# Inverting 64-wide blocks in a two-model kernel: five of its levels moved from pairs of 64-wide blocks to four blocks of 32 side by side

## The chip, the cores and the metric

One Trainium2 core runs the whole program in a single launch. Times are device microseconds (us). The profiled execution comes from the hardware profiler. In the text PE is TensorE, PEld its weight loads, DVE is VectorE, ACT ScalarE, POOL GpSimd.

## The reference

Two stacks follow each other on 256 tokens of width 2048, all in float32: two layers of four attention kinds, and then one layer with an RWKV-7 branch (16 heads of 64) and a gated-delta-rule branch (8 heads of 128), both run in two directions over 256 context tokens and 256 tokens, followed by gates, projections and an MLP. Only the two branches matter here. The delta rule of a chunk ends in a triangular solve:

```python
a_mat = jnp.einsum('bnhid,bnhjd->bnhij', kb, k) * decay
a_mat = jnp.where(idx[:, None] > idx[None, :], a_mat, 0.0) + jnp.eye(B_CHUNK, dtype=jnp.float32)
rhs = jnp.concatenate([v * beta[..., None], kb * jnp.exp(gc)[..., None]], axis=-1)
sol = lax.linalg.triangular_solve(a_mat, rhs, left_side=True, lower=True, unit_diagonal=True)
```

The RWKV branch has the same form once its scan is cut into chunks:

```python
# S_t = S_{t-1} diag(w_t) - (S_{t-1} kk_t) b_t^T + v_t k_t^T ;  y_t = S_t r_t
sa = jnp.einsum('bhvk,bhk->bhv', s, kk_t)
s = (s * dec_t[:, :, None, :] - sa[..., None] * b_t[:, :, None, :]
     + v_t[..., None] * k_t[:, :, None, :])
```

So the kernel needs, for each chunk of 128 tokens, the inverse of a unit triangular matrix of 128 by 128.

## The kernel before, in words

The program has five stages that follow one another, named in the code L (the first stack), P (the projections of the last layer), B (both branches), C (gates and output projection) and M (the MLP). Matrix products of L, P, C and M stream weights from memory; B works on what lies on the chip.

Stage B is made of threads: `thread_a(d)` for RWKV (eight pairs of heads, c = 0 to 7), `thread_b(d)` for the gated delta rule (eight heads h), each for the directions d = 0 and 1, and `tail_a`, `tail_b`, `base_a`, `base_b`. Each engine's program holds the same threads, and `weave.run` writes them out in turns: one step of each thread, up to its next `yield`, then the next step of each. So the order on every engine is fixed when the program is built, and an instruction that waits holds up all that stands behind it. Direction 1 of a head starts when direction 0 has done eight steps of its inverse (`weave.after(8, ...)`, `weave.until(("middle", c))`).

A step on PE leaves its result in a PSUM bank, taken in turn from the thread's ring (`DR`, two banks a direction; `ER`, one bank); DVE or ACT copies it out, and the thread's next step on PE waits for that.

`inverse` works level by level. The matrix is held as NA (its strict part, negated). X is the inverse of the diagonal blocks found so far, XP the transposed one. A level joins two blocks of width w = 1, 2, 4, ... 32 into one of 2w, and the last join makes 128. Matrices lie as n units: n = 8 for RWKV (4 chunks, 2 heads), n = 4 for the other. A unit of 128 by 128 has two diagonal blocks of 64; the upper is on partitions 0 to 63, the lower on 64 to 127, so that X takes 64 columns for each unit and all 128 partitions. The function `diagonal` issues the products of one call: for each unit and for each of the two halves a matmul 64 by 64 by 64. In the profile a float32 matmul is two MATMUL records and two LDWEIGHTS records. A level has three such calls:

- iq: NA times X. DVE then copies the wanted half of the columns into Q, under a mask (line 2146; line 2141 at level 0, whose copy goes into X at once).
- ix: XP and Q, which gives the new half of X; ACT copies it (line 1183).
- it: Q and XP, which gives the new half of XP; DVE copies it (line 2153).

POOL puts the identity back into the half of Q that DVE wrote (line 2747), with two Q buffers in turn. Level 0 has the first call alone, with an identity as right side. DVE starts an inverse by setting X and XP to the identity (line 2125) and writing the first level of XP under a mask (line 2132, one instruction for each half). Levels 0 to 5 give blocks of 64; level 6, with two calls of n matmuls each, joins them to 128 in the matrix XT, whose other blocks ACT (64 partitions) and POOL (line 2750) copy.

`region(buf, wd, side)` is the view of every second group of wd columns.

Of the kernel before, what the change touches and what calls it, by code (L numbers as in the profile page):

```python
# [35 lines left out]
for _n, _w in (("ident", 128), ("ones", 128), ("bones", 128), ("LE", 128), ("GT", 128), ("GE", 128), ("LT", 128),  # L36
               ("G1", 256), ("mask3", 384), ("permd", 128), ("permm", 128), ("Cd", 256), ("Sd", 256), ("Cm", 256),
               ("Sm", 256), ("scan", 512), ("type", 6), ("strict", 256), ("incl", 256), ("sel", 2), ("id64", 64)):
    CST[_n] = (CSTN, _w)
    CSTN += _w  # L40
MSK = {"strict": (0, 256), "incl": (256, 256), "lev": (512, 384), "xt0": (896, 64), "gla": (960, 1024)}
MSKN = 1984


def constants():
# [39 lines left out]
    ty = np.zeros((128, 6))  # L85
    for q in range(4):
        ty[:, q] = i % 4 == q
    for q in range(2):
        ty[:, 4 + q] = i % 2 == q
    put("type", ty)  # L90
    st = np.concatenate([a < b, a > b], 1)
    inc = np.concatenate([a <= b, a >= b], 1)
    put("id64", a[:, 0:1] % 64 == b[:, 0:64])
    put("sel", np.stack([i % 32 == 0, i % 32 == 1], 1))
# [5 lines left out]
    j = np.arange(32)  # L100
    r = i[:, None] % 64
    for d in range(2):
        for lv in range(6):
            w = 1 << lv
            s = (j // w) * 2 * w + d * w + j % w
            ok = (r // (2 * w) == s[None, :] // (2 * w)) & ((r // w) % 2 != (s[None, :] // w) % 2)
            m[:, 512 + (d * 6 + lv) * 32:512 + (d * 6 + lv) * 32 + 32] = ok
        tcol = 2 * j + 1 - d
        m[:, 896 + d * 32:896 + d * 32 + 32] = (r // 2 == tcol[None, :] // 2) & (r != tcol[None, :])
    for lv in range(7):  # L110
        w = 1 << lv
        m[:, 960 + lv * 128:960 + lv * 128 + 128] = (a // (2 * w) == b // (2 * w)) & ((a // w) % 2 == 0) & ((b // w) % 2 == 1)
    m[:, 960 + 896:960 + 1024] = a == b
# [126 lines left out]
def program(nc, W, WSM, LORA, PARd, CSTd, MSKd, CTX, XIN, XS, ZS, OUT):  # L240
    ctx = ExitStack()
    with ctx:
# [119 lines left out]
        with ExitStack() as st:  # L362
# [14 lines left out]
            for d in range(2):  # L377
                g = Mem()
                kb_ = alloc(1024)
                g.Kd, g.Bd = g.X, g.XP = kb_[:, 0:512], kb_[:, 512:1024]  # L380
                g.NA, g.AK, g.XT = alloc(1024), alloc(1024), alloc(1024)
                g.KK, g.Kt, g.Bt, g.RK, g.RB = [alloc(512) for _ in range(5)]
                g.Q = [alloc(512) for _ in range(2)]
# [11 lines left out]
            for d in range(2):  # L395
                g = Mem()
                g.NA, g.XT, g.dec, g.gl, g.Ke = [alloc(512) for _ in range(5)]
                g.X, g.XP = g.gl[:, 0:256], g.gl[:, 256:512]
# [5 lines left out]
            for d in range(2):  # L404
                g = G.d[d]
                g.Q = [alloc(256) for _ in range(2)]
# [4 lines left out]
            for g in R.d:  # L411
                g.Y, g.Rd = alloc(256), alloc(256)
            for g in R.d:
                g.H, g.R, g.U = [alloc(128) for _ in range(3)]
            for g in G.d:
                g.S, g.R, g.U = [alloc(128) for _ in range(3)]
            D.ab = alloc(128).rearrange("p (q n) -> p q n", q=4)
# [88 lines left out]
        def tensor(e):  # L506
# [307 lines left out]
            def inverse(tag, ring, NA, X, XP, Q, n):  # L814


                one = n == 4
                d = tag[-1]
                halves = [slice(0, 64), slice(64, 128)]
                me, other = halves[d], halves[1 - d]  # L820
# [15 lines left out]
                diagonal(bank(), NA, None, True).then_inc(*mark("pe_inv", "iq", tag, 0))  # L836
# [2369 lines left out]
```

## Time and profile before

| | us |
|---|---|
| median of 3 runs | 4343.27 |
| lowest, highest | 4336.54, 4343.53 |
| profiled execution | 4341.28 |
| its span | 4339.5 |
| PE busy (91% of the span) | 3936.5 |
| DVE, ACT, POOL busy | 1727.6, 1539.6, 1651.9 |

The page also cuts the span into 40 slices. Stage B lies at 2241 to 3335 us: there DMA is nearly at rest, and PE is busy for 955.6 of 1094 us.

Stage B repeats itself with a period of 133 us, in which two RWKV inverses and two of the other kind are made, one for each direction. Stage B holds 16 inverses of each kind.

### The profile page before, as it was taken

How to read it: one execution, taken by the hardware profiler on the slowest of the kernel's cores; microseconds unless marked ns; L12 is line 12 of the kernel's file. 1: busy time of each engine (PE TensorE's matmuls, PEld its weight loads, DVE VectorE, ACT ScalarE, POOL GpSimd, SP SyncE). 2: the span in 40 equal slices, each digit the busy share in tenths (PEclk: the TensorE clock that was granted, in tenths of full speed). 3: DMA queues.
4: the chain of work that ended last, by engine and by line, in shares of the span. 5: the costliest groups of instructions: out<-in, count | busy, mean ns of one | idle time of the engine just before them, and what ended most of it. 6: DMA issues, size and time to landing. Idle time of an engine off the chain costs nothing. (4 is left out here: it accounts for less than half of the span.)

```text
span 4339.5 us, 86947 instructions
## 1 busy us (share of the span) xinstructions
PE 3936.5 (91%) x37936; PEld 3563.3 (82%) x37936; DVE 1727.6 (40%) x3471; ACT 1539.6 (35%) x2630; POOL 1651.9 (38%) x1155
## 2 busy tenths in 40 slices
PE   7898998998897999999948889888898979999998
PEld 6898897887896777777737878877787979999998
DVE  2534433433433111112245565565654534333332
ACT  3333333333343222224423333333333434444442
POOL 1554453544451333335501111111112636666664
PEclk9999997999996999999969999999997979999999
DMA  4354452343442555567720000000002525555553
GB/s 154 136 184 156 165 198 105 136 175 134 153 161 95 210 206 196 216 215 271 260 72 25 25 11 16 25 24 25 6 2 112 203 95 185 181 186 179 185 184 127
DMA packets 115097, 585.17 MB, mean 135 GB/s; under 512 B 20768, under 2 KB 40096, under 8 KB 49952
## 3 DMA queue, kind: packets, MB, share of 16 engines
q1 hardware_dynamic: 114720, 579.62, 37.3%
q8 instruction: 301, 4.93, 0.5%
q14 instruction: 76, 0.62, 0.0%
HBM read 558.85 MB, written 20.71 MB: 134 GB/s over the span
## 5 line engine op out<-in xcount | busy, mean ns | idle before, releaser
L512 PE MATMUL bank<-act_L,part_L 128*128 128x256 f32 x7296 | 956.6, 291 | 1.9 <-DVE act_L L1805 1.9
L512 PEld LDWEIGHTS bank<-act_L,part_L 128*128 128x128 f32 x7296 | 916.2, 197 | 36.8 <-issue 27.5
L2639 POOL TENSOR_TENSOR part_L<-wring,part_L 128x512 fp32r<-128x512 f32 x304 | 532.6, 1753 | 657.1 <-ACT part_L L1183 656.7
L512 PE MATMUL bank<-act_P,part_P 128*128 128x512 f32 (+1 forms) x3488 | 723.2, 366 | 15.7 <-DVE act_P L2487 15.7
L512 PEld LDWEIGHTS bank<-act_P,part_P 128*128 128x128 f32 x3488 | 587.2, 188 | 176.0 <-issue 51.6
L512 PE MATMUL bank<-arena_B 64*64 64x64 f32 (+4 forms) x11456 | 542.8, 232 | 43.4 <-DVE arena_B L2255 18.5
L2639 POOL TENSOR_TENSOR part_M<-wring,part_M 128x512 fp32r<-128x512 f32 x256 | 457.3, 1797 | 307.5 <-ACT part_M L1183 307.5
L512 PEld LDWEIGHTS bank<-arena_B 64*64 64x64 f32 (+3 forms) x11456 | 469.2, 143 | 99.7 <-issue 21.7
L2639 POOL TENSOR_TENSOR part_P<-wring,part_P 128x512 fp32r<-128x512 f32 x184 | 328.3, 1789 | 471.0 <-ACT part_P L1183 471.0
L1800 DVE TENSOR_TENSOR part_L<-wring,part_L 128x512 fp32r<-128x512 f32 x304 | 219.9, 724 | 512.9 <-ACT part_L L1183 512.9
L1183 ACT ACTIVATE part_L<-wring 128x1024 fp32r<-128x1024 f32 x304 | 320.6, 1055 | 281.9 <-PE bank L512 265.3
L512 PE MATMUL bank<-act_h,part_M 128*128 128x256 f32 x3072 | 381.1, 287 | 22.8 <-DVE act_h L1805 22.8
L512 PEld LDWEIGHTS bank<-act_h,part_M 128*128 128x128 f32 x3072 | 376.3, 195 | 27.5 <-DVE act_h L1805 17.5
L512 PE MATMUL bank<-act_u,part_M 128*128 128x256 f32 x3072 | 369.3, 283 | 0.0
L512 PEld LDWEIGHTS bank<-act_u,part_M 128*128 128x128 f32 x3072 | 368.9, 192 | 0.0
L1183 ACT ACTIVATE part_M<-wring 128x1024 fp32r<-128x1024 f32 x256 | 270.2, 1057 | 267.4 <-PE bank L512 267.4
L1800 DVE TENSOR_TENSOR part_P<-wring,part_P 128x512 fp32r<-128x512 f32 x184 | 132.1, 718 | 497.1 <-ACT part_P L1183 497.1
L1800 DVE TENSOR_TENSOR part_M<-wring,part_M 128x512 fp32r<-128x512 f32 x256 | 182.2, 712 | 280.4 <-ACT part_M L1183 280.4
L1183 ACT ACTIVATE part_P<-wring 128x1024 fp32r<-128x1024 f32 x184 | 193.8, 1055 | 214.9 <-PE bank L512 214.9
L2644 POOL TENSOR_TENSOR smalls<-smalls,nhalf 128x2 f32<-128x2 f32 (+2 forms) x63 | 59.4, 943 | 378.3 <-DVE smalls L1788 378.2
L2747 POOL COPY arena_B<-cst 128x256 f32<-128x256 f32 (+1 forms) x96 | 38.0, 395 | 427.0 <-PE bank L512 427.0
L1183 ACT ACTIVATE arena_L<-bank 128x256 f32<-128x256 f32 (+2 forms) x177 | 70.6, 407 | 351.8 <-PE bank L512 291.1
(259 smaller groups left out, 4342.8 us busy)
## 6 DMA issues: line engine op xcount, KB each, us to landing
wring<-in_w SPq DMA_DIRECT2D x404, 1024.0 KB, 4.8
arena_P<-in_w SPq DMA_DIRECT2D x64, 1024.0 KB, 4.9
mring<-in_w SPq DMA_DIRECT2D x32, 1024.0 KB, 5.2
z_kept<-arena_P SPq DMA_DIRECT2D x34, 256.0 KB, 6.4
arena_B<-z_kept SPq DMA_DIRECT2D x34, 256.0 KB, 2.8
z_kept<-arena_P SPq DMA_DIRECT2D x58, 128.0 KB, 6.6
arena_C<-z_kept SPq DMA_DIRECT2D x32, 128.0 KB, 3.0
arena_B<-z_kept SPq DMA_DIRECT2D x26, 128.0 KB, 2.4
```

What stands on the lines that cost most here:

```text
L512: return e.matmul(out, lhsT, rhs, start=start, stop=stop)
L1183: return e.activation(out, a, ACT.Copy, scale=scale)
L1800: tt(wl[:, 0:4, :], wring[s % NS][:, 8 * j:8 * j + 4, :], wh[:, 0:4, :].bitcast(F32), sub).then_inc(*mark("dve_lo", "lov", stage, h))
L2639: e.tensor_tensor(wl[:, 4:8, :], wring[s % NS][:, 8 * j + 4:8 * j + 8, :], wh[:, 4:8, :].bitcast(F32), sub).then_inc(*mark("pool_lo", "lop ...
L2644: e.tensor_tensor(sm[:, 0:n], sm[:, 0:n], nhalf[:, 0:1].broadcast_to([128, n]), ALU.pow).then_inc(*mark("pool_root", "root", tag))
L2747: e.tensor_copy(region(Q[lv % 2], wd, d), same).then_inc(*mark(sem, "qf", tag, lv))
```

## The change

Levels 0 to 4, those whose blocks end at a width of 32, now work on the four diagonal blocks of 32 of a unit. Block k lies on partitions 32k to 32k+31, so X, XP and Q take 32 columns for each unit instead of 64 and still all partitions. `diagonal` is called with m = 32 and issues four matmuls of 32 by 32 by 32 for each unit, where it issued two of 64 by 64 by 64. Identity, masks and `region` are halved in width to match. Level 5 and the last join work on blocks of 64 as before, in buffers W and WP (the ones that X and XP had). After the copies of level 4, ACT writes X into W and DVE writes XP into WP with two instructions each: X times a column that is 1 on the partitions of the left block and 0 elsewhere, and the same for the right. Level 5 has a Q buffer of its own, Q5, whose identity half is never overwritten, so POOL's fifth copy is gone. The first level of XP is written by four instructions on 32 partitions each. The buffers' places in memory move with their sizes.

```diff
-                def diagonal(b, left, right, wide):
+                def diagonal(b, left, right, wide, m=32):
                     for u in range(n):
-                        for h in halves:
-                            lt = left[h, 128 * u + h.start:128 * u + h.stop] if wide else left[h, 64 * u:64 * u + 64]
-                            rt = C("id64")[h, :] if right is None else right[h, 64 * u:64 * u + 64]
-                            t = mm(b[h, 64 * u:64 * u + 64], lt, rt, True, True)
+                        for o in range(0, 128, m):
+                            h = slice(o, o + m)
+                            lt = left[h, 128 * u + o:128 * u + o + m] if wide else left[h, m * u:m * u + m]
+                            rt = C("id32")[h, :] if right is None else right[h, m * u:m * u + m]
+                            t = mm(b[h, m * u:m * u + m], lt, rt, True, True)
                     return t
...
                 for lv in range(1, 6):
+                    m, X, XP, Q = (32, g.X, g.XP, g.Q[lv % 2]) if lv < 5 else (64, g.W, g.WP, g.Q5)
...
-                    diagonal(b, NA, X, True).then_inc(*mark("pe_inv", "iq", tag, lv))
+                    diagonal(b, g.NA, X, True, m).then_inc(*mark("pe_inv", "iq", tag, lv))
...
-                    diagonal(b, XP, Q[lv % 2], False).then_inc(*mark("pe_inv", "ix", tag, lv))
+                    diagonal(b, XP, Q, False, m).then_inc(*mark("pe_inv", "ix", tag, lv))
                     b = bank()
-                    diagonal(b[:, 256:512] if one else b, Q[lv % 2], XP, False).then_inc(*mark("pe_inv", "it", tag, lv))
+                    diagonal(b[:, 256:512] if one else b, Q, XP, False, m).then_inc(*mark("pe_inv", "it", tag, lv))
```

On ACT:

```diff
-                    cp(region(X, wd, d), region(b[:, 0:64 * n], wd, d)).then_inc(*mark(sem, "free", ring.name, u))
+                    cp(region(X, wd, d), region(b[:, 0:m * n], wd, d)).then_inc(*mark(sem, "free", ring.name, u))
                     counts.at[("X", tag, lv)] = counts.last(sem)
+                    if lv == 4:
+                        w.wait_ge(last(sem))
+                        for j in range(2):
+                            t = cp(g.W.rearrange("p (u j s) -> p u j s", j=2, s=32)[:, :, j, :], X.rearrange("p (u s) -> p u s", s=32),
+                                   C("side")[:, j:j + 1])
+                        t.then_inc(*mark(sem, "wide", tag))
+                        counts.at[("X", tag, 4)] = counts.last(sem)
```

On DVE:

```diff
-                for h in (0, 64):
-                    hs = slice(h, h + 64)
+                for h in range(0, 128, 32):
+                    hs = slice(h, h + 32)
...
-                    e.tensor_copy(region(XP, wd, 1 - d), region(bx, wd, 1 - d)).then_inc(*mark(sem, "free", ring.name, u))
+                    e.tensor_copy(region(XP if lv < 5 else g.WP, wd, 1 - d), region(bx, wd, 1 - d)).then_inc(*mark(sem, "free", ring.name, u))
                     counts.at[("XT", tag, lv)] = counts.last(sem)
+                    if lv == 4:
+                        own(sem)
+                        for j in range(2):
+                            t = ts(g.WP.rearrange("p (u j s) -> p u j s", j=2, s=32)[:, :, j, :], XP.rearrange("p (u s) -> p u s", s=32),
+                                   C("side")[:, j:j + 1], None, mult, None)
+                        t.then_inc(*mark(sem, "widep", tag))
+                        counts.at[("XT", tag, 4)] = counts.last(sem)
```

On POOL:

```diff
-                    w.wait_ge(done("it", tag, lv))
-                    e.tensor_copy(region(Q[lv % 2], wd, d), same).then_inc(*mark(sem, "qf", tag, lv))
+                    if lv < 5:
...
+                        w.wait_ge(done("it", tag, lv))
+                        e.tensor_copy(region(g.Q[lv % 2], wd, d), same).then_inc(*mark(sem, "qf", tag, lv))
```

What the rows below name: `bank` is PSUM; `arena_B`, `wring`, `xT` and `cst` are memory in which stage B keeps its buffers. PE in the last period of stage B, from the last call of level 0 on, before:

```order
L512 MATMUL bank<-cst,arena_B 64x64 [waits s_dve_rwkv]
L512 MATMUL bank<-cst,arena_B 64x64 x15
L512 MATMUL bank<-wring,arena_B 64x64 [waits s_dve_gdn]
L512 MATMUL bank<-wring,arena_B 64x64 x7
L512 MATMUL bank<-arena_B,wring 64x64 x8
L512 MATMUL bank<-arena_B,cst 128x128 [waits s_act_rwkv]
L512 MATMUL bank<-arena_B 128x128
L512 MATMUL bank<-wring,arena_B 128x128
L512 MATMUL bank<-cst,arena_B 128x128 [waits s_act_gdn]
L512 MATMUL bank<-xT,cst 128x128 x2
L512 MATMUL bank<-arena_B 64x64 [waits s_dve_rwkv]
L512 MATMUL bank<-arena_B 64x64 x15
```

and after the change:

```order
L514 MATMUL bank<-cst,arena_B 32x32 [waits s_dve_rwkv]
L514 MATMUL bank<-cst,arena_B 32x32 x31
L514 MATMUL bank<-cst 32x32 [waits s_dve_gdn]
L514 MATMUL bank<-cst 32x32 x31
L514 MATMUL bank<-arena_B,cst 128x128 [waits s_act_rwkv]
L514 MATMUL bank<-arena_B 128x128
L514 MATMUL bank<-wring,arena_B 128x128
L514 MATMUL bank<-cst,arena_B 128x128 [waits s_act_gdn]
L514 MATMUL bank<-xT,cst 128x128 x2
L514 MATMUL bank<-wring,arena_B 32x32 [waits s_dve_rwkv]
L514 MATMUL bank<-wring,arena_B 32x32 x31
L514 MATMUL bank<-arena_B 64x64 [waits s_dve_gdn,s_act_gdn]
```

The calls stand in the same places; those of levels 0 to 4 have twice the matmuls (32 for 16, 64 for 32, and for n = 4, 32 for 16), and the level-5 call of the other thread, 64 by 64, now stands between calls of 32 by 32.

ACT at the end of the last RWKV inverse, levels 3, 4 and 5 and the last join, before (the view's last numbers are groups by width):

```order
L1183 ACTIVATE arena_B<-bank 128x32x8 [waits s_pe_inv]
L1183 ACTIVATE cst<-bank,cst 128x128 [waits s_pe_chain]
L1183 ACTIVATE wring<-bank 128x128 [waits s_pe_chain]
L1183 ACTIVATE arena_B<-bank 128x16x16 [waits s_pe_inv]
L1183 ACTIVATE cst<-bank,cst 128x128 [waits s_pe_chain]
L1183 ACTIVATE arena_B<-bank 128x8x32 [waits s_pe_inv]
L1183 ACTIVATE arena_B<-bank 64x512 [waits s_pe_inv]
L1183 ACTIVATE arena_B<-arena_B 64x8x64 [waits s_dve_rwkv]
```

and after:

```order
L1187 ACTIVATE wring<-bank 128x16x8 [waits s_pe_inv]
L1187 ACTIVATE cst<-bank,cst 128x128 [waits s_pe_chain]
L1187 ACTIVATE wring<-bank 128x128 [waits s_pe_chain]
L1187 ACTIVATE wring<-bank 128x8x16 [waits s_pe_inv]
L1187 ACTIVATE arena_B<-wring,cst 128x8x32 [waits s_act_rwkv]
L1187 ACTIVATE arena_B<-wring,cst 128x8x32
L1187 ACTIVATE cst<-bank,cst 128x128 [waits s_pe_chain]
L1187 ACTIVATE arena_B<-bank 128x8x32 [waits s_pe_inv]
L1187 ACTIVATE arena_B<-bank 64x512 [waits s_pe_inv]
L1187 ACTIVATE arena_B<-arena_B 64x8x64 [waits s_dve_rwkv]
```

The copies of levels 3 and 4 have half the columns (8 units by 16 where 16 groups by 16 stood), and two instructions of 128 by 256 stand behind the level-4 copy, the first of which waits for that copy.

DVE has the like on its own line: behind its level-4 copy two instructions of line 1800, each 128 by 8 by 32, write WP, ahead of the chain instruction that stood behind the copy (line 2405, line 2386 before). At the start of that inverse its program has four instructions of 32 by 128 (line 2142) where two of 64 by 256 stood (line 2132).

## Rows read from the trace of the kernel before

**Rows 1.** The page: busy time, PE by slice, the chain by engine.

```profile
PE 3936.5 (91%) x37936; PEld 3563.3 (82%) x37936; DVE 1727.6 (40%) x3471; ACT 1539.6 (35%) x2630; POOL 1651.9 (38%) x1155
...
PE   7898998998897999999948889888898979999998
...
PE 22%; issue 1%; DVE 1%; ACT 1%; POOL 0%; POOLq 0%; DVEq 0%; ACTq 0%
```

**Rows 2.** One period in windows: us, busy (x instructions) of each engine, clock, DMA share, GB/s.

```profile
2428.70:2464.00 35.30, 25.66 (x338) 22.72 (x335) 26.51 (x64) 12.17 (x29) 4.94 (x7) 0.81 0.04 13
2464.00:2496.00 32.00, 31.24 (x621) 28.79 (x621) 15.15 (x37) 9.84 (x29) 4.25 (x8) 1.00 0.24 66
2496.00:2530.00 34.00, 29.11 (x474) 24.86 (x472) 24.38 (x58) 11.77 (x30) 4.16 (x6) 1.00 0.01 2
2530.00:2561.70 31.70, 31.46 (x697) 28.57 (x695) 10.79 (x32) 10.52 (x30) 5.51 (x12) 1.00 0.01 4
```

**Rows 3.** What PE waited for in 2241 to 3335 us: us in total, times, longest us.

```profile
PE bank L512 <- DVE cst L2380: 36.9, 16, 4.5
PE bank L512 <- ACT wring L1180: 19.5, 7, 3.3
...
PE bank L512 <- DVE arena_B L2141: 11.6, 16, 2.0
...
PE bank L512 <- DVE arena_B L2146: 9.5, 9, 1.3
```

**Rows 4.** Groups by shape, 2241 to 3335 us: first and last of six with 64*64.

```profile
L512 PE MATMUL bank<-arena_B 64*64 64x64 f32 x10240 | 374.4, 222 | 22.9 <-DVE arena_B L2141 11.6 <-DVE arena_B L2146 9.5 <-ACT arena_B L1183 1.7
...
L512 PE MATMUL bank<-arena_B,xT 64*64 64x64 f32 x384 | 15.2, 218 | 0.0
```

**Rows 5.** Timeline from 2496 us: start, length, engine, line, shapes, count, [idle, releaser].

```profile
2496.31 1.15 PE L512 MATMUL bank<-arena_B 64*64 64x64 f32 x32
...
2497.50 0.43 DVE L2146 COPY_PREDICATED arena_B<-msk,bank 128x256 f32<-128x256 uint8 x1 [1.89 <-PE bank L512]
...
2499.52 1.94 PEld L512 LDWEIGHTS bank<-arena_B 64*64 64x64 f32 x64 [0.76 <-issue]
...
2504.82 2.08 PE L512 MATMUL bank<-arena_B 64*64 64x64 f32 x64 [1.29 <-DVE arena_B L2146]
```

**Rows 6.** The same timeline: PE, products of 128 columns, 2 and 8 records.

```profile
2506.83 0.49 PE L512 MATMUL bank<-cst,arena_B 128*128 128x128 f32 x2
...
2507.69 1.16 PE L512 MATMUL bank<-cst,arena_B 128*128 128x128 f32 x8 [0.38 <-DVE arena_B L1788]
```

**Rows 7.** Timeline at 2177 us: products and loads with 32 columns of weights each.

```profile
2177.48 0.16 PEld L512 LDWEIGHTS bank<-arena_P 128*32 128x32 f32 x8 [5.35 <-DMA arena_P<-in_w]
2177.49 1.41 PE L512 MATMUL bank<-arena_P 128*32 128x512 f32 x8 [4.44 <-DMA arena_P<-in_w]
```

**Rows 8.** Groups by shape, 2241 to 3335 us: copies, scalings, products of 512 columns.

```profile
L2153 DVE COPY arena_B<-bank 128x256 f32<-128x256 f32 x80 | 33.8, 423 | 144.1 <-PE bank L512 144.1
...
L1183 ACT ACTIVATE arena_B<-bank 128x256 f32<-128x256 f32 x80 | 30.7, 384 | 47.2 <-PE bank L512 47.2
...
L2132 DVE COPY_PREDICATED arena_B<-msk,arena_B 64x256 f32<-64x256 uint8 x32 | 23.3, 729 | 1.0
L2153 DVE COPY arena_B<-bank 128x128 f32<-128x128 f32 x80 | 23.3, 291 | 36.5 <-PE bank L512 36.5
...
L1183 ACT ACTIVATE arena_B<-bank 128x128 f32<-128x128 f32 x80 | 22.4, 280 | 150.0 <-DVE arena_B L2153 150.0
...
L512 PE MATMUL bank<-arena_B 128*128 128x512 f32 x32 | 16.4, 592 | 0.0
...
L1788 DVE TENSOR_SCALAR arena_B<-cst,arena_B 128x128 f32<-128x128 f32 x64 | 15.1, 300 | 0.0
...
L2132 DVE COPY_PREDICATED arena_B<-msk,arena_B 64x128 f32<-64x128 uint8 x32 | 14.6, 455 | 1.1
...
L1788 DVE TENSOR_SCALAR arena_B<-arena_B 128x512 f32<-128x512 f32 x32 | 12.1, 415 | 1.7 <-ACT arena_B L1180 1.7
```

More of the change, by code:

```diff
@@ L405, in program @@
                 g = G.d[d]
-                g.Q = [alloc(256) for _ in range(2)]
+                g.Q5 = alloc(256)
                 g.AT, g.qs, g.O = [alloc(256) for _ in range(3)]
@@ L812, in inputs, with inverse @@
                     yield from project_p(n)
-            def inverse(tag, ring, NA, X, XP, Q, n):
+            def inverse(tag, ring, g, n):
+                d = tag[-1]
                 one = n == 4
-                d = tag[-1]
-                halves = [slice(0, 64), slice(64, 128)]
-                me, other = halves[d], halves[1 - d]
+                me, other = slice(64 * d, 64 * d + 64), slice(64 - 64 * d, 128 - 64 * d)
                 def bank():
@@ L981, in thread_a @@
                     yield from scores(c, d)
-                    yield from weave.after(8, ("middle", c) if d == 0 else None, inverse((c, d), DR[d], g.NA, g.X, g.XP, g.Q, 8))
+                    yield from weave.after(8, ("middle", c) if d == 0 else None, inverse((c, d), DR[d], g, 8))
                     yield from chain(c, d)
@@ L1059, in thread_b @@
                     w.wait_ge(done("qse", h, d))
-                    yield from weave.after(8, ("middleb", h) if d == 0 else None, inverse(("g", h, d), ring, g.NA, g.X, g.XP, g.Q, 4))
+                    yield from weave.after(8, ("middleb", h) if d == 0 else None, inverse(("g", h, d), ring, g, 4))
                     w.wait_ge(done("XT", ("g", h, d), 6))
@@ L1540, in thread_a @@
                     yield from scores(c, d)
-                    yield from weave.after(8, ("middle", c) if d == 0 else None, inverse((c, d), DR[d], g.X, g.XP, g.XT, 8, "act_rwkv"))
+                    yield from weave.after(8, ("middle", c) if d == 0 else None, inverse((c, d), DR[d], g, 8, "act_rwkv"))
                     yield from chain(c, d)
@@ L1609, in thread_b @@
                     weave.said.add(("prepb", h, d))
-                    yield from weave.after(8, ("middleb", h) if d == 0 else None, inverse(("g", h, d), ring, g.X, g.XP, g.XT, 4, "act_gdn"))
+                    yield from weave.after(8, ("middleb", h) if d == 0 else None, inverse(("g", h, d), ring, g, 4, "act_gdn"))
                     for i, q in enumerate(ORDER[d]):
@@ L2765, in thread_a @@
                         yield
-                    for lv, old in ((-1, 5), (0, 4)):
+                    for lv, old in ((-1, 3), (0, 4)):
                         counts.at[("qf", (c, d), lv)] = counts.at[("qf", (c - 1, d), old) if c else ("qid", d)]
-                    yield from weave.after(8, ("middle", c) if d == 0 else None, inverse((c, d), g.XP, g.XT, g.Q, 8, "pool_rwkv"))
+                    yield from weave.after(8, ("middle", c) if d == 0 else None, inverse((c, d), g, 8, "pool_rwkv"))
                     for _ in range(12):
@@ L2810, in thread_b @@
                     weave.said.add(("prepb", h, d))
-                    for lv, old in ((-1, 5), (0, 4)):
+                    for lv, old in ((-1, 3), (0, 4)):
                         counts.at[("qf", ("g", h, d), lv)] = counts.at[("qf", ("g", h - 1, d), old) if h else ("gqid", d)]
-                    yield from weave.after(8, ("middleb", h) if d == 0 else None, inverse(("g", h, d), g.XP, g.XT, g.Q, 4, "pool_gdn"))
+                    yield from weave.after(8, ("middleb", h) if d == 0 else None, inverse(("g", h, d), g, 4, "pool_gdn"))
                     for _ in range(12):
```

112 lines of the change are left out of this document (58 added, 54 removed).

## The prediction

> **What bounds the kernel now.** I read the page first, then stage B by windows, then what PE waits for there, and last the single calls. The page: PE is busy 91% of the span and the chain that ended last runs mostly over PE [rows 1]. So a change counts for what it takes from PE, or for the waits that it makes PE meet. In the slices PE is at eight or nine tenths nearly everywhere, stage B (slices 21 to 31) included, where the change lies.
>
> One period of stage B in windows shows two kinds of stretch [rows 2]. In the second and the fourth, 63.7 of 133 us, PE is busy 62.7 us, that is 98%, and they hold 1318 of the period's some 2130 matmul records, 62%. In the other two PE is at 73% and 86%. So PE's own work sets the pace in the larger part, and in the rest it waits in turn for DVE and ACT: over stage B most for DVE's line 2380 and ACT's line 1180, which are not in the inverse, while the inverse's own copies, lines 2141 and 2146, end only 21.1 us of waits [rows 3].
>
> **What one matmul record costs now.** The busy column of the groups ends each group with a pipeline tail, so I take differences. A call of 32 records (64 by 64) is 1.15 us long and one of 64 is 2.08 us [rows 5]: 0.93 / 32 = 29.1 ns for a record. The two halves of the array share that: records of 128 columns, one tile at a time, differ by (1.16 - 0.49) / 6 = 112 ns [rows 6]. With 64 columns and two tiles a pair takes 58.2 ns. From 112 to 58.2 the columns halve: (112 - 58.2) / 64 = 0.84 ns a column and 4.4 ns fixed.
>
> **How many records.** An inverse issues 16 calls of 2n matmuls and two of n, 34n; with 16 inverses of n = 8 and 16 of n = 4 that is 34 x 192 = 6528 matmuls, 13056 records, of which the first row of the group has 10240 [rows 4]. Levels 0 to 4 are 13 of the calls: 26 x 192 = 4992 matmuls, 9984 records, 9984 x 29.1 ns = 290.5 us of PE. The change makes them 19968. It gains if a record falls below 290.5 / 19968 = 14.5 ns, and the whole case hangs on that number.
>
> **The price of a 32 by 32 record.** No row has one, so it is bounded from both sides.
> - Lower end: four quarters at once, each at 32 x 0.84 + 4.4 = 31.3 ns, thus 7.8 ns a record. That four tiles can run at once is seen at 2177 us: eight products with 32 weight columns and 512 moving columns take 1.41 us together, and eight weight loads 0.16 us [rows 7], where a product of 512 columns on the whole array takes 16.4 / 32 = 0.51 us, eight of them 4.1 us [rows 8]. And the eight loads together span 0.16 us, so starts can follow each other by some 7 ns at least for eight records.
> - Upper end: nothing gained from smaller tiles. The nearest row with as many records in a run is the 64 by 64 one, 29.1 ns [rows 5].
> I take 10 ns, near the lower end, since rows 7 are the only ones with four tiles and they come near to four at once; above the end, because eight records are a burst and a call now has 64 or 128 in a row, each with its load.
>
> **The terms.**
> - PE in levels 0 to 4: 19968 x 10 ns = 199.7 us for 290.5: -90.8 us of busy time. The ends: -134.8 at 7.8 ns, +290.6 at 29.1.
> - How much of it reaches the end: all of it in the two full windows, 62% of the records [rows 2], and a fifth of the rest, where DVE and ACT pace. 0.62 + 0.08 = 0.7: -63.6 us.
> - Copies of half the columns: ACT 280 ns for 384, DVE 291 for 423 [rows 8]. In the full windows they are hidden: the copy of line 2146 ends at 2497.93 and PE first loads weights of the next call at 2499.52 [rows 5], 1.6 us of other threads' matmuls later. I take them as what keeps that slack open while PE gets shorter, and at 0.
> - Widening on ACT: two copies of 128 by 256, 2 x 384 = 768 ns for n = 8 and 2 x 280 for n = 4 [rows 8]; on DVE two scalings between 300 and 415 ns each [rows 8]. X and XP of level 4 come later by at most some 0.75 us, less the 0.1 that their copies got shorter. Behind them on ACT and DVE stand the chain's copies of the other direction, for which PE waits too. With the slack of 1.6 us most is hidden. From 0 to 32 x 0.67 = 21 us; I take 8.
> - Start of an inverse on DVE: four instructions for two, but each of 128 elements for 256, thus 4 x 455 for 2 x 729 ns, +362 ns for n = 8 [rows 8]. This one is not hidden: PE waits 16 times for line 2141 behind it, 11.6 us in all [rows 3]. Against it stand the identity copies and the level-0 copy, both at half width, each shorter by 0.1 us or more. From -3 to +6 us over 16 inverses; I take +2.
> - POOL: four copies of half the width for five; PE never waits for POOL's line 2747, 0.
> Sum: -63.6 + 8 + 2 = -53.6. From the profiled execution, 4341.3 (span 4339.5 and 1.8 around it), to 4287.7; the median of the runs shown is 2.0 above the profiled one, so 4290.
>
> **Two rules against it.** Rows 5 show two row tiles writing one bank side by side at 29.1 ns a record. The Trainium skill, TensorEngine Tiling (Array Packing), section Restrictions and Gotchas, says that different row tiles cannot access one PSUM bank at the same time; all four quarters write one bank here. The trace does not bear it out for two tiles; by the rule a record would cost a full 31.3 ns, and the change would lose more than its upper end.
>
> Rows 7 show starts some 7 ns apart. The Trainium skill, TensorE: Matmul & The Clock Gate, section "Wait — 56ns, not 53.3ns?", says that from start to start of two matmuls it is never under about 25 ns, however few the columns. If that held for records on different tiles in a long run, 19968 x 25 = 499 us, an estimate from that page, would stand for 290.5, and the time would be some 4520. The burst speaks against it, no row of a long run does.
>
> **The rivals.**
> - *A floor for each record (slower).* PE's supply of loads and matmuls, not the array, sets the pace once the tiles are small. It decides from 14.5 ns a record on. At 29.1 ns: +290.6 us, of which I count 0.85, since more PE work also fills PE's idle time: +247 + 10, so 4600. At 20 ns: (399.4 - 290.5) x 0.8 + 10 = +97, so 4440. For it: the longest runs of records are at 29.1, never below [rows 5]. Against it: rows 7, and that 58.2 ns for a pair of tiles is what 64 columns cost by the slope, so that the array alone explains it. Chance 0.22.
> - *Latency takes the gain.* With shorter calls the slack of 1.6 us closes, PE meets the round trip over DVE and ACT in every level, and the widening is paid in full: a quarter of -90.8 is kept, -23, and +21 +2 on the other side: 0, so 4343. For it: PE already waits 1.29 us for line 2146 in the window that DVE fills [rows 5]. Against it: the full windows, where PE never idles [rows 2]. From 4315 to 4350, most of it below. Chance 0.20.
> - *The forecast* at 7.8 to 12 ns. At 7.8: -134.8 x 0.8, plus 2, so 4237; at 12: (239.6 - 290.5) x 0.7 + 10 = -26, so 4317. Chance 0.58.
>
> **How the numbers follow.** No change can be told here within 0.2%, 8.7 us. Faster: 0.55 of the forecast's 0.58, and 0.10 of the latency case's 0.20: 0.65. Same: 0.02, 0.06 and the low end of the floor case 0.01: 0.09. Slower: 0.01, 0.04 and 0.21: 0.26. The range goes from 4235, the lower end of the unknown price, to 4390, which takes in the latency case and the floor up to some 17 ns; the floor above that, about 0.15, is left out. The likeliest case's own range is 4237 to 4317.
>
> **What the profile after would show.** Calls of n = 8 with 64 records of 32 by 32: a length of some 0.8 us where 32 records had 1.15 says that the price was right; 1.0 or more says floor. PE busy in stage B down by 90 us from 955, with DVE's and ACT's waits for PE shorter. If latency took it: PE busy is down as much, but waits of PE for lines 2146 and 2153 (2158 and 2165 after) grow far above 10 us and the full windows are gone. If widening counts: PE waits at level 5 for ACT's and DVE's last writes of level 4. Stages L, P, C and M should keep their times within some us. The forecast is wrong if a record of 32 by 32 costs more than 14.5 ns, or if PE's granted clock, 1.00 in the full windows [rows 2], falls to its lower level there with the smaller tiles.

## The result: 4439 us, slower by 2.2%

The changed kernel takes 4439.2 us (median of 4 runs, 4429.9 to 4446.7) where the kernel before takes 4343.4 in the same comparison: the ratio is 1.0223, 95% interval 1.0200 to 1.0246. The forecast was 4290 with a range up to 4390. The time is that of the rival "a floor for each record", at the 20 ns that it was also worked out for (4440).

The page of the changed kernel, the lines that answer to [rows 1], and its line on the queue that brings the engines' instructions (packets, MB, share of 16 engines):

```profile
span 4445.0 us, 107047 instructions
...
PE 3954.1 (89%) x47920; PEld 3561.0 (80%) x47920; DVE 1713.7 (39%) x3599; ACT 1550.9 (35%) x2694; POOL 1633.4 (37%) x1127
...
PE   7898998988898999999668888888887989999998
...
q8 instruction: 379, 6.21, 0.6%
```

PE has 9984 matmul records more, as worked out, but its busy time grew by 18 us, where the forecast had levels 0 to 4 take 91 us less of it. Queue q8 has 379 packets where the kernel before has 301.

The windows of the kernel before, for what lies ahead of stage B and for stage B (columns as in [rows 2]):

```profile
0.00:2241.00 2241.00, 2019.86 (x13324) 1755.06 (x13324) 731.09 (x1328) 772.10 (x1179) 931.13 (x571) 0.94 0.48 174
2244.00:3337.00 1093.00, 952.58 (x16785) 849.53 (x16784) 611.84 (x1499) 356.38 (x944) 149.16 (x263) 0.92 0.07 18
```

The same two windows of the changed kernel:

```profile
0.00:2241.00 2241.00, 2020.80 (x13303) 1756.40 (x13303) 729.87 (x1326) 771.11 (x1179) 929.99 (x574) 0.94 0.48 174
2244.00:3443.00 1199.00, 969.53 (x26783) 846.49 (x26784) 599.97 (x1630) 369.35 (x1008) 131.73 (x232) 0.81 0.07 19
```

Up to 2241 us nothing differs. Stage B is 1199 us long for 1093, and these 106 us are the whole difference of the two profiled spans (4445.0 and 4339.5; the medians differ by 96). In it PE stands idle for 229 us instead of 140, and its granted clock is 0.81 instead of 0.92.

What PE waited for in stage B of the changed kernel, 2244 to 3440 us, the longest sums (us in total, times, longest us), with the first row of its weight loads last; this answers to [rows 3]:

```profile
PE bank L514 <- issue: 88.2, 75, 2.6
PE bank L514 <- DVE cst L2399: 35.2, 16, 4.4
PE bank L514 <- DVE arena_B L2274: 17.2, 8, 2.4
PE bank L517 <- DVE wring L2240: 14.1, 8, 1.9
PE bank L514 <- ACT wring L1184: 11.1, 7, 2.0
PE bank L514 <- DVE arena_B L2158: 10.4, 8, 1.8
PE bank L514 <- DVE cst L2153: 8.2, 8, 1.0
```

```profile
PEld bank L514 <- issue: 146.8, 240, 2.7
```

The first row is new: 75 gaps, 88.2 us, in which PE waits for nothing that the profile shows. The kernel before has no such row for PE at all, and 38.0 us for its weight loads. The other rows changed little and both ways: line 2399 (2380 before) 35.2 us for 36.9, lines 2153 and 2158 of the inverse (2141 and 2146 before) 24.3 for 21.1, with 5.7 of them under another name, ACT's line 1184 (1180 before) 11.1 for 19.5. Without the 88.2 us PE idles 141 us in stage B, where it idled 140 before: the new gaps are all of the added idle time.

The timeline of the changed kernel shows short calls without a gap and such gaps inside a call (start, length, engine, line, shapes, count, [idle before, releaser]):

```profile
2499.41 0.45 PE L514 MATMUL bank<-cst,arena_B 32*32 32x32 f32 x32
...
2506.35 0.75 PE L514 MATMUL bank<-wring,arena_B 32*32 32x32 f32 x64
...
2509.42 1.15 PE L514 MATMUL bank<-wring 32*32 32x32 f32 x109
2511.68 0.37 PE L514 MATMUL bank<-wring 32*32 32x32 f32 x19 [1.12 <-issue]
...
2518.60 1.13 PE L514 MATMUL bank<-wring 32*32 32x32 f32 x106
2520.38 0.39 PE L514 MATMUL bank<-wring 32*32 32x32 f32 x22 [0.64 <-issue]
...
2524.26 1.31 PE L514 MATMUL bank<-wring 32*32 32x32 f32 x128
```

64 records take 0.75 us and 128 take 1.31: (1.31 - 0.75) / 64 = 8.8 ns a record. So in such a call a record takes even less than the 10 ns of the forecast. But two calls that belong together, ix and it with 64 records each, are cut after 109 and after 106 of the 128, by 1.12 and 0.64 us. From one of these gaps to the other PE waits for no other engine.

### The profile page after: what moved, and what is told of

Read it like the earlier page. It is cut to its first block and busy times, and to the rows that moved or that the text cites. A ratio compares the mean times of both kernels' runs of the same rounds, so it can differ in the third digit from the quotient of the medians.

```text
span 4445.0 us, 107047 instructions
## 1 busy us (share of the span) xinstructions
PE 3954.1 (89%) x47920; PEld 3561.0 (80%) x47920; DVE 1713.7 (39%) x3599; ACT 1550.9 (35%) x2694; POOL 1633.4 (37%) x1127
## 5 line engine op out<-in xcount | busy, mean ns | idle before, releaser
L1187 ACT ACTIVATE part_L<-wring 128x1024 fp32r<-128x1024 f32 x304 | 320.2, 1054 | 284.3 <-PE bank L514 267.9
L514 PE MATMUL bank<-arena_B 64*64 64x64 f32 (+7 forms) x4096 | 347.9, 268 | 46.4 <-DVE arena_B L2274 17.2
L514 PEld LDWEIGHTS bank<-arena_B 64*64 64x64 f32 (+4 forms) x4096 | 281.5, 169 | 88.1 <-issue 25.8
L514 PE MATMUL bank<-cst,arena_B 32*32 32x32 f32 (+2 forms) x4264 | 209.8, 226 | 80.6 <-DVE cst L2399 35.2
L1187 ACT ACTIVATE part_P<-wring 128x1024 fp32r<-128x1024 f32 x184 | 193.6, 1054 | 215.1 <-PE bank L514 215.1
L514 PEld LDWEIGHTS bank<-cst,arena_B 32*32 32x32 f32 (+2 forms) x4264 | 158.9, 134 | 108.8 <-DVE cst L2399 36.7
```

Source lines behind the costliest of these rows:

```text
L514: return e.matmul(out, lhsT, rhs, start=start, stop=stop)
L1187: return e.activation(out, a, ACT.Copy, scale=scale)
```

## The experiments

Two theories. "A record" is a MATMUL record, and each comes with one LDWEIGHTS record, so that "a pair" is a load with its matmul. *Supply*: PE gets its instructions by queue q8 in packets, so many per unit of time, and a stretch with more loads and matmuls than that stands still. *Latency*: the inverse's steps became short against the round trip over DVE and ACT. All medians of the kernel before in the comparisons lie between 4338.8 and 4343.4.

The last column leaves out one load's wait of 10.5 to 11.2 us for the first product of stage C, which stands at the edge of stage B in every kernel.

| kernel | median us | ratio to before [95%] | stage B us | clock in B | PE records in B | PE / PEld idle for "issue" us |
|---|---|---|---|---|---|---|
| before | 4343.4 | 1 | 1093 | 0.92 | 16785 | 0 / 38.0 |
| changed | 4439.2 | 1.0223 [1.0200, 1.0246] | 1199 | 0.81 | 26783 | 88.2 / 146.8 |
| e1_split | 4427.4 | 1.0205 [1.0185, 1.0225] | 1175 | 0.91 | 26767 | 50.3 / 103.4 |
| e2_pairunits | 4247.6 | 0.9783 [0.9768, 0.9797] | 1007 | 0.88 | 17574 | 5.6 / 50.2 |
| e3_gdn_only | 4352.5 | 1.0026 [1.0014, 1.0039] | 1097 | 0.89 | 20120 | 2.1 / 42.5 |
| e4_rwkv_only | 4405.2 | 1.0146 [1.0131, 1.0161] | 1150 | 0.88 | 23447 | 57.6 / 107.6 |
| e6_transpose | 4278.3 | 0.9863 [0.9843, 0.9882] | 1019 | 0.87 | 20634 | 33.0 / 80.5 |
| e7b_transpose0 | 4279.4 | 0.9861 [0.9843, 0.9880] | 1032 | 0.84 | 19101 | 25.6 / 81.8 |
| e8b_transpose_dead | 4432.5 | 1.0211 [1.0194, 1.0228] | 1199 | 0.81 | 26786 | 83.5 / 144.6 |
| e9_transpose_wide | 4301.1 | 0.9906 [0.9889, 0.9923] | 1054 | 0.88 | 20633 | 15.8 / 61.5 |
| e10_after_wide | 4429.9 | 1.0208 [1.0188, 1.0228] | 1190 | 0.88 | 26785 | 59.3 / 111.6 |

**e1_split.** The kernel before, with the products of levels 0 to 4 cut in two, so that it has the changed kernel's number of records and nothing else of the change.

```diff
-                            t = mm(b[h, 64 * u:64 * u + 64], lt, rt, True, True)
+                            m = 64 // parts
+                            for j in range(parts):
+                                t = mm(b[h.start + m * j:h.start + m * j + m, 64 * u:64 * u + 64], lt[:, m * j:m * j + m], rt, True, True)
```

> The kernel before, with each matmul of levels 0 to 4 (64 by 64 by 64) cut into two of 32 weight columns each. The PE instructions are as many as after the change (19968 records in levels 0 to 4), all else (blocks, buffers, copies) is as before. Theory supply: PE gets its instructions in packets of 256 at 3.2 us or more each; calls of small records outrun them, PE stalls, and the granted clock falls with the stalls. Then this kernel is slow too: 4400 to 4480, with some 70 to 110 us of issue stalls in stage B. Rival small tiles: the loss comes from the 32 by 32 tiles or from the widening instructions; then 4343 plus or minus 15.

4427.4 us, 84 above the kernel before. Its windowed row of stage B:

```profile
2244.00:3419.00 1175.00, 993.42 (x26767) 865.98 (x26766) 612.94 (x1499) 355.61 (x944) 147.44 (x262) 0.91 0.06 18
```

Cutting a product in two costs the array nothing in itself. Calls of 32, 64 and 128 of the cut records on the timeline:

```profile
2543.31 0.65 PE L512 MATMUL bank<-cst,arena_B 64*32 64x64 f32 x32
...
2519.98 1.17 PE L512 MATMUL bank<-arena_B 64*32 64x64 f32 x64
...
2516.82 1.99 PE L512 MATMUL bank<-arena_B 64*32 64x64 f32 x128
```

That is (1.99 - 0.65) / 96 = 14.0 ns a record where a record of the kernel before takes 29.1. So the array has no more to do than before, and copies, masks and waits are as before. The 9984 records more cost 84 us all the same: in stage B PE is busy for 41 us more and idle for 41 us more. The latency, the widening and the 32 by 32 tiles are not needed for a loss of this size. The clock, which the expectation had fall, hardly moved (0.91 for 0.92).

**e2_pairunits.** The changed kernel, with one product for two units in levels 1 to 4. The second unit of each pair is multiplied with the first one's weights, so those results are not the inverse's.

```diff
-                    for u in range(n):
+                    k = 2 if m == 32 and right is not None else 1
+                    for u in range(0, n, k):
...
-                            t = mm(b[h, m * u:m * u + m], lt, rt, True, True)
+                            t = mm(b[h, m * u:m * (u + k)], lt, rt, True, True)
```

> The changed kernel, but in levels 1 to 4 one matmul streams the 64 columns of two units with the weights of the first, so half the units get a wrong product. PE instructions there are as many as before the change; blocks of 32, widening, DVE's four starting instructions stay. Theory supply: the stalls go (under 20 us of issue in stage B), the clock comes back to 0.93 or so, 4330 to 4360. Rival widening or small tiles: still above 4400.

4247.6 us: 192 us below the changed kernel for 9216 records fewer (21 ns each), and 96 below the kernel before. Both are better than I had expected (4330 to 4360), although the clock, 0.88, did not come back to the 0.93 that I had put there; part of the 21 ns is the clock, as shown below. The steps of DVE, ACT and POOL are those of the changed kernel, the widening too. So what the change added on the other engines costs little, and with few instructions the blocks of 32 gain.

**e3_gdn_only and e4_rwkv_only.** Blocks of 32 only for the delta rule's inverses (n = 4), or only for RWKV's (n = 8); the other kind keeps the code before.

```diff
-                    yield from weave.after(8, ("middle", c) if d == 0 else None, inverse((c, d), DR[d], g, 8))
+                    yield from weave.after(8, ("middle", c) if d == 0 else None, inverse_old((c, d), DR[d], g.NA, g.X, g.XP, g.Q, 8))
```

> Blocks of 32 only in the gated delta rule's inverses (n = 4), the RWKV ones as before. A third of the added records (3328). Theory supply: a level of both threads has 384 instructions for 288 before and 576 after the change, near what the supply gives in a level's 5.6 us: stalls of 20 us or less, and 37 us of PE time saved, 4320 to 4355. Rival, loss in proportion to records or to widenings: a third (records) of the 96 us, 4375, or half (widenings), 4391.

> Blocks of 32 only in the RWKV inverses (n = 8), the others as before: 6656 of the 9984 added records. Theory supply: 480 instructions a level, above the supply: 50 to 70 us of stalls, 4370 to 4420. Rival in proportion: two thirds of 96 us, 4407 (records), or half, 4391 (widenings).

Of 9984 more records, n = 4 has 3328 and n = 8 has 6656. The first cost 9 us, 2.8 ns each, the second 62 us, 9.3 ns each. Together they cost 71 of the 96 us: the loss grows faster than the count. Where a call is 32 records and stands between wide products, PE meets almost no new gaps (2.1 us); where ix and it make 128 records in a row, it does (57.6 us). The gaps don't explain e3_gdn_only to the end: its expectation had 37 us of array work saved, and no gain came. Its clock is 0.89 for 0.92.

**e5_burst.** The kernel before, and at the start of stage B, with nothing to wait for: 1024 products of 32 by 32, 1024 of 64 by 64, and again 1024 of 32 by 32 (two records each).

```diff
+            for m, k in ((32, 1024), (64, 1024), (32, 1024)):
+                for i in range(k):
+                    o = m * i % 128
+                    h = slice(o, o + m)
+                    mm(banks[7][h, m * (i // 4 % 4):m * (i // 4 % 4) + m], ident[h, o:o + m], ident[h, o:o + m], True, True)
```

> The kernel before, with three runs of matmuls that wait for nothing at the start of stage B, into a free bank: 1024 of 32 by 32 by 32 over the four quarters, 1024 of 64 by 64 by 64 over the two halves, and again 1024 of 32 by 32 by 32. Theory supply: the first records run at 8 to 9 ns, then PE gets 256 instructions in 3.2 to 3.5 us, so a long run of 32 by 32 settles at 25 to 27 ns a record (1024 matmuls in 51 to 56 us), in spurts with stalls of 2 us between; 64 by 64 goes at its 29.2 ns without stalls. Rival array: 9 ns a record throughout, 18 us. Of the clock: if small tiles lower it, it falls in the 32 by 32 runs and is back in the 64 by 64 one.

4499.4 us in a single run. The timeline of its burst on PE:

```profile
2218.12 1.93 PE L512 MATMUL bank<-cst 32*32 32x32 f32 x128 [1.81 <-issue]
...
2221.59 1.93 PE L512 MATMUL bank<-cst 32*32 32x32 f32 x128 [1.54 <-issue]
...
2225.34 1.93 PE L512 MATMUL bank<-cst 32*32 32x32 f32 x128 [1.81 <-issue]
...
2247.29 62.60 PE L512 MATMUL bank<-cst 64*64 64x64 f32 x2176 [1.42 <-issue]
2311.56 1.65 PE L512 MATMUL bank<-cst 32*32 32x32 f32 x128 [1.67 <-issue]
2315.03 1.93 PE L512 MATMUL bank<-cst 32*32 32x32 f32 x128 [1.82 <-issue]
```

And its instruction queue in 2311 to 2364 us, then its windows of one stretch of each kind (the last of them the same 53 us):

```profile
q8 instruction: 14, 0.23, 1.7%
```

```profile
2216.00:2231.00 15.00, 8.02 (x535) 7.35 (x526) 0.00 (x0) 0.00 (x0) 0.00 (x0) 0.50 0.02 4
2250.00:2280.00 30.00, 30.00 (x1024) 30.00 (x1022) 0.00 (x0) 0.00 (x0) 0.00 (x0) 0.99 0.02 4
2311.00:2364.00 53.00, 27.57 (x1853) 25.65 (x1856) 0.00 (x0) 0.00 (x0) 0.00 (x0) 0.51 0.02 4
```

This is the supply by itself. 128 matmuls and their 128 loads run off in 1.93 us, then PE stands still. In the second run of 32 by 32 a spurt starts 3.47 to 4.02 us after the last one, 3.69 in the mean: 28.8 ns for a load with its matmul. Spurts of 256 instructions fit the packets: e1_split has 19968 PE instructions and 78 packets more than the kernel before, 256 in each. In 53 us q8 brought 14 packets, 3.8 us each, and in the trace each spurt of that stretch starts 2.2 to 2.6 us after a packet of q8 did. The row of 62.60 us is the 64 by 64 run with the first 132 records of the next run merged into it, so its price is read from a stretch that holds nothing else: 1024 records in 30.00 us, 29.3 ns, without a gap. That is the array's price and the supply's at once, and neither [rows 5] nor this row can tell which of them sets it.

**e6_transpose.** Since both are products of the same matrices, the new XP is the transposed new X. VectorE makes it with one 32 by 32 block transpose, and PE does not issue `it` at levels 1 to 4.

```diff
-                    b = bank()
-                    diagonal(b[:, 256:512] if one else b, Q, XP, False, m).then_inc(*mark("pe_inv", "it", tag, lv))
+                    if lv == 5:
+                        b = bank()
+                        diagonal(b[:, 256:512] if one else b, Q, XP, False, m).then_inc(*mark("pe_inv", "it", tag, lv))
...
+                    if lv < 5:
+                        w.wait_ge(done("Xc", tag, lv))
+                        e.transpose(XP, X).then_inc(*mark(sem, "XT", tag, lv))
```

> The changed kernel, but at levels 1 to 4 the matmul step it (Q with XP) is gone: VectorE makes the new XP as one 32 by 32 block transpose of the new X, after ScalarE's copy. TensorE issues 9 instead of 13 calls of 4n records in levels 0 to 4 of an inverse: 13824 records instead of 19968, so 6144 loads and 6144 matmuls fewer, some 48 fetch packets of 256 instructions. Theory (supply of instructions): the pairunits kernel took away 9216 pairs (4 of the levels) and 192 us, 21 ns per pair, so 6144 pairs are worth 110 to 130 us: 4310 to 4330, below the kernel before by 10 to 35 us, and the gaps of TensorE with no wait shrink from 235 us (both rows) to about 130. Rival 1 (only the array's time counts): 6144 x 9 ns = 55 us, 4385. Rival 2 (the chain of an inverse's steps sets the pace, which now goes from X by ScalarE to XP by VectorE in series): no gain, or slower, 4440 or more, with more waiting of TensorE for VectorE in the inverse.

4278.3 us, 161 below the changed kernel and 1.4% below the kernel before. That is 26 ns for each of the 6144 pairs of a load and a matmul, three times the array's 8.8 and more than the expectation had (4310 to 4330). It is not a clean price of an instruction: the clock went from 0.81 to 0.87 with it. Its rows of the transposes (groups by shape, mean ns in the second column) and of its stage B:

```profile
L2165 DVE STREAM_TRANSPOSE wring<-wring 128x256 f32<-128x256 f32 x64 | 28.4, 444 | 91.3 <-ACT wring L1187 91.1
...
L2165 DVE STREAM_TRANSPOSE cst<-cst 128x128 f32<-128x128 f32 x64 | 19.7, 308 | 24.5 <-ACT cst L1187 23.8
```

```profile
2244.00:3263.00 1019.00, 831.36 (x20634) 717.98 (x20634) 608.07 (x1629) 369.95 (x1008) 131.90 (x231) 0.87 0.07 21
```

VectorE waits longer for ACT there. For PE that has a small price: its waits for the inverse (ACT's line 1187 in `arena_B` and DVE's two copies behind iq) come to 42.9 us, for 31.4 in the changed kernel.

**e8b_transpose_dead.** e6_transpose, with the removed matmuls put back, their results read by nobody.

```diff
+                    if lv < 5:
+                        diagonal(b[:, 256:512], Q, XP, False, m)
                     diagonal(b, XP, Q, False, m).then_inc(*mark("pe_inv", "ix", tag, lv))
```

> The kernel of e6_transpose, but TensorE also issues the matmuls that it had taken away, into columns 256 to 511 of the bank of the step beside them, ahead of those; nobody reads their result. So VectorE's transposes and the waits are as in e6_transpose, and TensorE's instructions as in the changed kernel. Theory (supply): the time is back near the changed kernel's, 4410 to 4440, with TensorE's gaps with no wait back over 200 us in both rows. Rival (e6_transpose won by its waits or by VectorE's work): close to e6_transpose plus the array's 55 us, 4280 to 4335.

4432.5 us, back at the changed kernel's time, with nearly the same gaps (83.5 and 144.6 us) and the same clock, 0.81. So e6_transpose won by what PE no longer issues, not by DVE's work or by shorter waits. At 8.8 ns the array's part of that is 54 of the 161 us.

**e7b_transpose0.** e6_transpose, and at level 0 X as the transposed XP as well.

```diff
-                diagonal(bank(), g.NA, None, True).then_inc(*mark("pe_inv", "iq", tag, 0))
...
+                e.transpose(X, XP).then_inc(*mark(sem, "X", tag, 0))
```

> The kernel of e6_transpose, and at level 0 too TensorE does nothing: X is made as VectorE's 32 by 32 block transpose of XP, in place of the copy of the identity, the matmuls with the identity and the predicated copy. 3072 loads and 3072 matmuls fewer (24 fetch packets). Theory (supply): e6_transpose took 6144 pairs away and the median fell by 161 us, 26 ns per pair; 3072 pairs at the pairunits kernel's 21 ns and at 26 ns are 65 to 80 us: 4200 to 4215. Rival 1 (only the array's time): 3072 x 9 ns = 28 us, 4250. Rival 2 (what e6_transpose won came from the shorter wait for XP or from VectorE's work, and not from TensorE's instructions; or TensorE's gaps by now come from other stages): 4265 to 4285, no change.

The expectation counted the records wrong: level 0 has 1536, not 3072 (the trace has 1533 fewer), so supply wanted some 35 us, and even the array's price 13. Measured: 4279.4, no difference. Its stage B:

```profile
2244.00:3276.00 1032.00, 840.96 (x19101) 727.81 (x19101) 605.38 (x1597) 369.78 (x1008) 131.40 (x232) 0.84 0.07 21
```

PE is busy 10 us more with 1533 records fewer, at a clock of 0.84 for 0.87. The largest group of 128 by 128 by 128 products, which the edit does not touch, went from 328 to 340 ns each. So the records saved seem to be given back as slower array work; of e6_transpose this is the fastest of four executions, of e7b_transpose0 one near its median. What made the clock fall there, no run tells. This miss stands against a pure price per instruction.

**e9_transpose_wide and e10_after_wide.** All but the last unit's products of levels 1 to 4 stream 64 moving columns for 32, in e6_transpose and in the changed kernel; the next unit's product overwrites the second half. The instructions stay the same in number and order, the array has 54 or 81 us more to do.

```diff
-                            rt = C("id32")[h, :] if right is None else right[h, m * u:m * u + m]
-                            t = mm(b[h, m * u:m * u + m], lt, rt, True, True)
+                            k = 64 if right is not None and u < n - 1 else m
+                            rt = C("id32")[h, :] if right is None else right[h, m * u:m * u + k]
+                            t = mm(b[h, m * u:m * u + k], lt, rt, True, True)
```

> The kernel of e6_transpose, but the matmuls of levels 1 to 4 stream 64 moving columns instead of 32 (all but the last unit's); the second half of each result is overwritten by the next unit's product. TensorE's instructions are the same in number and order, the array does twice the columns. In the pairunits kernel a record of 64 columns on a quarter costs (1.10 - 0.65) / 32 = 14.1 ns in a run, and one of 32 columns 8.8 ns in the changed kernel. So the array has 12288 x 0.83 x 5.3 ns = 54 us more to do. Theory (supply of instructions, some 27 ns for a load and a matmul in long runs): a part of that hides where TensorE would stand still for want of instructions: 4278 + 15 to 35, 4290 to 4315. If the granted clock answers to how much the array is used, it also rises above 0.87 in stage B and takes some more off, to 4270 at best. Rival (the array's time counts in full): 4325 to 4335.

> The changed kernel with the same edit: 64 moving columns instead of 32 in levels 1 to 4, all but the last unit's, the same instructions in number and order. The array has 18432 x 0.83 x 5.3 ns = 81 us more to do. Theory (supply): most of it hides in the gaps for want of instructions, 88 us of TensorE's and more in its loads, so between 4430 and 4470; with a higher clock than the changed kernel's 0.81 in stage B it may come out below 4439, to 4410 at best. Rival (the array's time counts in full): 4510 to 4520.

e9: 4301.1, 23 us more for an estimated 54 of array work. e10: 4429.9, 9 us less than the changed kernel in the median, for an estimated 81 us more of array work; the two intervals overlap, so it is no gain, but it is far from the 4510 that array time would give. Stage B of e10_after_wide:

```profile
2244.00:3434.00 1190.00, 996.36 (x26785) 879.23 (x26784) 600.54 (x1630) 369.76 (x1008) 132.84 (x232) 0.88 0.07 19
```

The added columns filled gaps: PE is idle for 194 us where it was for 229. And the clock is 0.88 for 0.81. So two things covered the 81 us, and this run alone doesn't show that the gaps would have done it.

**What the clock costs.** The rows give a size for it. One group of PE's products that no edit touches, with the same 256 records each time, before, in e1_split, changed and in e10_after_wide:

```profile
L512 PE MATMUL bank<-wring,arena_B 128*128 128x64 f32 x256 | 42.0, 289 | 0.4 <-ACT wring L1183 0.4
...
L512 PE MATMUL bank<-wring,arena_B 128*128 128x64 f32 x256 | 40.9, 282 | 1.6 <-issue 1.3 <-ACT wring L1185 0.4
...
L514 PE MATMUL bank<-wring,arena_B 128*128 128x64 f32 x256 | 46.9, 313 | 0.4 <-ACT wring L1187 0.4
...
L514 PE MATMUL bank<-wring,arena_B 128*128 128x64 f32 x256 | 42.4, 291 | 0.4 <-ACT wring L1188 0.4
```

All groups of stage B but the 64 by 64 and the 32-wide ones, some 3740 records in each kernel, have busy columns that add up to 601 us before, 612 in e1_split, 683 in the changed kernel, 684 in e8b_transpose_dead, 637 in e10_after_wide, 623 in e6_transpose, 652 in e7b_transpose0 and 629 in e3_gdn_only. The ends of neighbouring groups overlap in these sums, so a difference is a size and not an exact share of the stage. The changed kernel's 82 us more go with its clock, the 11 of e1_split with a clock that hardly moved. The same sums go a long way with three results above. In e10_after_wide 46 us come back by the clock and 36 by filled gaps, about the 81 us of added work. In e7b_transpose0 28 us are lost against e6_transpose, where the missing records should have gained 13 to 35. In e3_gdn_only 28 us are lost against the kernel before, where 37 should have been gained. Why the clock fell to 0.81 with 32 columns a record and stood at 0.88 with 64, with the same instructions, no run tells.

## Why the prediction was wrong

- **The first term failed**, "PE in levels 0 to 4: 19968 x 10 ns = 199.7 us for 290.5: -90.8 us of busy time". Its price was right for one call: "I take 10 ns, near the lower end", and a call's records take 8.8 ns; by the prediction's own test (64 records in 0.8 us; they took 0.75) all was well. The step that failed took what a burst costs as what a long stretch costs, and put the supply of instructions at nothing in this term. Stage B grew by 106 us, so that the 19968 records came to (290.5 + 106) / 19968 = 19.9 ns each, if all the loss is put on them.
- **The bound.** The text saw the danger ("eight records are a burst and a call now has 64 or 128 in a row, each with its load") and dismissed it with "the array alone explains" 58.2 ns for a pair of tiles, 29.1 ns a record. But e5_burst shows the supply at 28.8 ns a pair of load and matmul in the mean, the very same place. In its longest runs of 64 by 64 the kernel before was already at the pace that the supply gives, which its rows couldn't show. Smaller tiles make such a run no faster, and here they doubled its instructions.
- **The break-even of 14.5 ns** has the right sign with 19.9 ns, but that is no test of it: both come from the same 290.5 us.
- **PE busy down by 90 us**: it went from 952.6 to 969.5 us in stage B, with 89 us of idle time on top. The idle time is the gaps of supply. That the busy time did not fall is in part the clock: the lower of its two levels, 1.2 GHz, held for some 455 us of stage B where before it held for some 170, and the products that the change doesn't touch took 82 us more. The prediction named the clock's fall in the full windows as a thing that would make it wrong, and priced it nowhere; in 2500 to 2533 us it was still 1.00, the fall came in other stretches. How the 106 us divide between supply and clock isn't separated. That supply alone can make such a loss is shown by e1_split, 82 us of stage B at a clock of 0.91; but at 14.0 and 8.8 ns a record the changed kernel's array has some 100 us less to do than e1_split's, and it is the slower one.
- **Widening +8, start +2**: not measured one by one. e2_pairunits has them all and is 96 us faster than the kernel before, so they are not where the loss is.
- **Latency rival**: not what happened. It wanted PE's busy time down by as much as the forecast and the waits for lines 2158 and 2165 far above 10 us. Busy time rose, line 2158 ends 10.4 us of waits for 9.5 and line 2165 none that the view lists. In e6_transpose, where XP comes later, PE's waits for the inverse's copies grew by some 12 us and the kernel won 161.
- **Floor rival**: this was it, with its mechanism (supply of loads and matmuls) and its place, and its chance of 0.22 was too low. That its time at 20 ns, 4440, is the measured one is partly luck: 20 ns was a value for trial that no row gave. The supply's price in a long run is 28.8 ns, a short call meets less of it, and the average of 19.9 ns holds a fall of the clock that the rival didn't have.
- **The two rules.** Four quarters writing one bank take (0.75 - 0.45) / 32 = 9.4 ns a record (calls of 64 and of 32 records, each in one bank), and 8.8 where a stretch of 128 goes on into a second bank; one tile after the other would take 31.3. The Trainium skill, TensorEngine Tiling (Array Packing), section Restrictions and Gotchas, which forbids different row tiles one PSUM bank at the same time, is not borne out by this. Starts that follow by some 9 ns also go below the 25 ns of the Trainium skill, TensorE: Matmul & The Clock Gate, section "Wait — 56ns, not 53.3ns?"; only the average of a long run, 28.8 ns, looks like it, and that one goes with the packets.

## What to carry to other kernels

Count PE's instructions, loads included, beside its columns: here a long stretch is fed one load with its matmul every 28.8 ns in the mean, so in a long run products whose array time is under that gain nothing from being made smaller, and more of them lose. Short calls between wide products are another matter (e3_gdn_only: 2.1 us of gaps). "Issue" as the releaser of PE, together with more packets on the instruction queue, is how it looks in a profile; a short call that runs faster says nothing about it. Read the granted clock beside it: it can take back a saving in products that nobody changed. Then look for instructions to remove: a transposed result that another engine can write (e6_transpose: 4278 us, with e7b_transpose0 the fastest kernel here that computes the whole result). One product over two units would remove more (e2_pairunits), but no kernel here does that and gets the right result.

## What was not expected of the hardware

- PE's instructions come in packets of 256. When PE waits for nothing else a new spurt starts every 3.5 to 4.0 us (e5_burst, second run); its 128 records are done in 1.93 us at 1.2 GHz.
- In such a starved run the granted clock is 0.51, where 30 us with the array busy all the time had 0.99 (e5_burst): short of instructions, PE also ran at its lower level.
- 81 us more of array work (an estimate), with the instructions unchanged, cost nothing (e10_after_wide, 4429.9 for 4439.2): part of it filled gaps, and the clock of 0.88 for 0.81 made the other products faster.
- A float32 transpose of 32 by 32 blocks on VectorE, 128 by 256, takes 444 ns, near the copy of the same size out of PSUM, 423 [rows 8].
